# A hybrid encoder layer on one core: grouped FFN-up products, a quarter-wise opening, another VectorE order at the output projection, and 14 zero products on TensorE

## The chip, the cores and the metric

One core of a Trainium2 chip runs the whole program. The metric is device time in microseconds. Three runs of the kernel before gave 1219.9, 1220.18 and 1221.23 us, so its median is 1220.18 us.

## What is computed

One layer (`DEPTH = 1`) over 256 tokens of width 2048, everything in f32:

```python
h = x
u = rmsnorm(h, norm_mix)
p_mla, p_ssm, p_swa = split(u @ w_in)                       # 2048 -> 3660
h = h + concat([mla_mixer(p_mla), mamba2_mixer(p_ssm), swa_mixer(p_swa)]) @ w_out   # 2048 x 2048
q = rmsnorm(h, norm_cross) @ cross_wq                       # 4 heads of 128
k, v = rmsnorm(mem, norm_mem) @ cross_wkv                   # 256 memory tokens, 2048 -> 1024
h = h + softmax(q k^T / sqrt(128)) v @ cross_wo
g, val = split(causal_dwconv(rmsnorm(h, norm_ffn) @ ffn_w_up))   # 2048 -> 2 x 5632
h = h + (silu(g) * val) @ ffn_w_down                        # 5632 -> 2048
return rmsnorm(h, norm_final)
```

## The kernel before

**Products.** A weight slab is 1 MB: 128 partitions by 2048 f32 columns. SyncE loads it into one of three slots of `raw`; ScalarE rounds it into `hi` (the helper `split`, L382); VectorE takes the rest `lo = raw - hi` (L775); TensorE then works in fp32r. The activations have the same two parts, `ux[:, k, 0]` = `uh` and `ux[:, k, 1]` = `ul`. A product is three passes: hi by uh, hi by ul, lo by uh (`three`, L1326 to L1331, 256 or 512 columns each). In the FFN-up product (`wide_product`) the first two are one matmul of 512 columns, since `uh` and `ul` of a k lie side by side:

```python
pe.matmul(bank[b][:, :], wh, both_, start=(k == 0), stop=False)      # L1353, 512 columns
pe.matmul(bank[b][:, 0:T], wl, uh[:, k, :], start=False, stop=False) # L1354, 256 columns
```

for 16 values of k; the last k has them in the other order (L1356, L1357). A tile waits for `lo_ready` of its slab, which VectorE gives.

**Order.** It is written out by hand on every engine, with semaphores between them; the slabs are numbered (`N_XK` 0 to 3 the keys' weights, `N_XV` 4 to 7 the values', then `w_in`, `N_OUT` 41 to 56, `N_WQ`, `N_WO`, `N_FFN` from 65). On each engine the code for slab n is followed by the `split` of slab n+2.

**The opening.** `mem` comes in four loads of 512 columns, and the key weights as four slabs of one head each, (2048 rows by 128 columns: 512-byte rows in DRAM). SyncE waits for all four quarters of `mem` before it issues slabs 1 to 3, then 15 loads of vectors and tables, x (two loads of 1 MB), the positions, four small parameter loads, and the value slabs. TensorE turns `mem` by transposes (`turn_group`, L1377: 8 groups of 4), ScalarE and VectorE scale the turned groups into `uh` and `ul` (`token_hi` L430, `token_lo` L817), and TensorE makes the four key tiles one after the other (48 matmuls of 256 columns each), then the four value products. Behind each value product it turns two groups of x (`turn_scaled`, L1396), for which it needs `x_diag`, the root of x's squares. VectorE takes each key when it is done (`take_key`, L904) and makes the rotary angles (L919 to L938, 19 operations that wait for one another) after the last key.

**The output projection.** 16 slabs; the product of slab `N_OUT` (41) lies in banks 2 and 3, and the product of slab `N_OUT+4` wants the same banks, so it waits until `add_mixed(N_OUT, ...)` on VectorE (L1131, signal `mix_added`) has taken them. `sum_tiles` (L824) adds the squared tiles with a `tensor_reduce` over a strided view.

**The FFN.** 11 groups of 8 up tiles and 4 down products. An up tile's bank is taken by ScalarE (`up_low`, L730) and VectorE (L1254, L1255, signal `fconv_raw`); tile c waits for `fconv_raw` of tile c-2, since banks 0 and 1 alternate. The first take also needs `hf_scale` (L1218), which VectorE copies when TensorE has spread it (`spread_scale`, L1403, signal `hf_spread`) between the first two tiles.

## Time and profile before

| | us |
|---|---|
| median of 3 runs | 1220.18 |
| the profiled execution | 1220.99 |
| its span, first to last instruction | 1219.2 |
| TensorE busy | 1187.8 (97%) |
| VectorE busy | 896.8 (74%) |
| ScalarE busy | 655.0 (54%) |
| read from HBM | 214.33 MB, 178 GB/s over the span |
| mean granted clock | 0.994 |

The profile is of one execution. "Busy" counts the instructions of an engine, not its waits; a matmul's shown length is longer than the step from its start to the next one's start, because matmuls are pipelined, so the pace is read from the starts. 1.00 of the granted clock is 2.4 GHz and 0.50 is 1.2 GHz. The 1.8 us between the span and the execution's time lie around the program.

### The profile page before, as it was taken

What the parts mean: (1) busy time and instruction counts of PE and PEld (TensorE: products, weight loads), DVE (VectorE), ACT (ScalarE), POOL (GpSimd) and SP (SyncE); (2) the same over time, 40 slices, a digit from 0 to 9 for tenths busy, and PEclk for the clock granted to TensorE, in tenths of its full rate; (3) what the DMA queues carried; (4) which work ended last, traced back from release to release, by engine and by line L of the source; (5) the groups of instructions that cost most, each with busy time, mean ns of one, the idle gap of its engine ahead of it and who ended that gap; (6) DMA issues with size and microseconds to landing.
All of it is one profiled execution on the core that took longest, in us unless ns stands there. A gap on an engine that the chain in (4) does not pass through costs nothing.

```text
span 1219.2 us, 18801 instructions
## 1 busy us (share of the span) xinstructions
PE 1187.8 (97%) x6960; PEld 1037.7 (85%) x6960; DVE 896.8 (74%) x1257; ACT 655.0 (54%) x866; POOL 0.2 (0%) x4
## 2 busy tenths in 40 slices
PE   6899999999999999999999999999999999999996
PEld 6799999988878978888888888888888888888885
DVE  6753998778676667877767767777777677777777
ACT  6544764475644557545555555555454555555454
POOL 0000000000000000000000000000000000000000
PEclk9999999999999999999999999999999999999998
DMA  9676766432565445675765758575757657575751
GB/s 278 231 170 173 184 162 173 126 108 70 207 207 173 144 153 158 202 207 173 198 181 173 204 162 217 172 206 172 206 172 198 180 175 203 164 215 172 207 173 70
DMA packets 309358, 217.11 MB, mean 178 GB/s; under 512 B 11350, under 2 KB 272190, under 8 KB 308670
## 3 DMA queue, kind: packets, MB, share of 16 engines
q1 hardware_dynamic: 309134, 216.31, 60.8%
q8 instruction: 33, 0.54, 0.2%
q10 hardware_dynamic: 176, 0.14, 0.1%
q14 instruction: 15, 0.12, 0.0%
HBM read 214.33 MB, written 2.10 MB: 178 GB/s over the span
## 4 chain that ended last, share of the span: by engine, by line
PE 91%; DVE 3%; ACT 2%; DMA 1%; SPq 1%; issue 1%; ACTq 0%; DVEq 0%
PE bank L1353 25%; PE bank L1354 13%; PE bank L1326 9%; PE bank L1328 9%; PE bank L1327 9%; PE bank L1329 6%; PE bank L1330 6%; PE bank L1331 6%; PE bank L1357 2%; PE bank L1435 1%; DVE lo L775 1%; ACT hi L382 1%; PE bank L1466 1%; PE bank L1356 1%; DMA raw<-in_cross_wkv_dram 1%
## 5 line engine op out<-in xcount | busy, mean ns | idle before, releaser
L775 DVE TENSOR_TENSOR lo<-raw,hi 128x2048 fp32r<-128x2048 f32 x195 | 446.6, 2290 | 135.4 <-ACT hi L382 127.6
L1353 PE MATMUL bank<-ux,hi 128*128 128x512 f32 x1320 | 470.1, 399 | 1.3 <-DVE arena L1255 1.3
L382 ACT CAST hi<-raw 128x2048 fp32r<-128x2048 f32 x195 | 371.5, 1910 | 112.2 <-PE bank L1328 104.0
L1354 PE MATMUL bank<-ux,lo 128*128 128x256 f32 x1320 | 370.7, 281 | 0.0
L1353 PEld LDWEIGHTS bank<-ux,hi 128*128 128x128 f32 x1320 | 248.1, 188 | 59.0 <-issue 1.6
L1354 PEld LDWEIGHTS bank<-ux,lo 128*128 128x128 f32 x1320 | 249.3, 189 | 4.0
L1326 PE MATMUL bank<-hi,ch 128*128 128x512 f32 x464 | 181.4, 391 | 1.4 <-DVE cl L1193 1.4
L1328 PE MATMUL bank<-hi,cl 128*128 128x512 f32 x464 | 180.2, 388 | 0.0
L1327 PE MATMUL bank<-lo,ch 128*128 128x512 f32 x464 | 180.1, 388 | 0.0
L1329 PE MATMUL bank<-ux,hi 128*128 128x256 f32 (+1 forms) x592 | 170.5, 288 | 2.8 <-DVE lo L775 2.6
L1330 PE MATMUL bank<-ux,hi 128*128 128x256 f32 (+1 forms) x592 | 167.4, 283 | 0.0
L1331 PE MATMUL bank<-ux,lo 128*128 128x256 f32 (+1 forms) x592 | 167.3, 283 | 0.0
L730 ACT COPY arena<-bank 128x256 f32<-128x256 f32 x88 | 32.9, 374 | 210.2 <-PE bank L1357 210.2
L1329 PEld LDWEIGHTS bank<-ux,hi 128*128 128x128 f32 (+1 forms) x592 | 112.6, 190 | 6.5 <-DVE lo L775 2.8
L1330 PEld LDWEIGHTS bank<-ux,hi 128*128 128x128 f32 (+1 forms) x592 | 112.7, 190 | 0.1
L1331 PEld LDWEIGHTS bank<-ux,lo 128*128 128x128 f32 (+1 forms) x592 | 112.7, 190 | 0.0
L1326 PEld LDWEIGHTS bank<-hi,ch 128*128 128x128 f32 x464 | 87.1, 188 | 19.3 <-DVE cl L1193 1.8
L1234 DVE SCALAR_TENSOR_TENSOR arena<-arena,vecs 128x255 f32<-128x255 f32 (+1 forms) x176 | 85.1, 484 | 24.4 <-DVE arena L1234 3.6
L1328 PEld LDWEIGHTS bank<-hi,cl 128*128 128x128 f32 x464 | 87.1, 188 | 18.1
L1327 PEld LDWEIGHTS bank<-lo,ch 128*128 128x128 f32 x464 | 87.2, 188 | 17.8
L1254 DVE TENSOR_TENSOR arena<-bank,arena 128x256 f32<-128x256 f32 x88 | 37.2, 423 | 64.2 <-ACT arena L730 63.5
L1170 DVE TENSOR_TENSOR arena<-arena,bank 128x512 f32<-128x512 f32 x96 | 61.0, 682 | 0.7 <-PE bank L1328 0.7
(239 smaller groups left out, 1060.5 us busy)
## 6 DMA issues: line engine op xcount, KB each, us to landing
raw<-in_ffn_w_up_dram SPq DMA_DIRECT2D x88, 1024.0 KB, 5.8
raw<-in_ffn_w_down_dram SPq DMA_DIRECT2D x44, 1024.0 KB, 5.1
raw<-in_w_in_dram SPq DMA_DIRECT2D x28, 1024.0 KB, 5.6
raw<-in_w_out_dram SPq DMA_DIRECT2D x16, 1024.0 KB, 5.2
raw<-in_cross_wkv_dram SPq DMA_DIRECT2D x7, 1024.0 KB, 8.8
arena<-in_x_dram SPq DMA_DIRECT2D x4, 1024.0 KB, 5.9
raw<-in_cross_wq_dram SPq DMA_DIRECT2D x4, 1024.0 KB, 5.4
raw<-in_cross_wo_dram SPq DMA_DIRECT2D x4, 1024.0 KB, 5.1
```

What stands on the lines that cost most here:

```text
L382: a.mark(act.copy(hi[:, n % RING, :], raw[:, n % RING, :]), S("hi_ready"))
L775: d.mark(dve.tensor_tensor(lo[:, n % RING, :], raw[:, n % RING, :], hi[:, n % RING, :].bitcast(F32), ALU.subtract), S("lo_ready"))
L1170: d.mark(dve.tensor_tensor(hres[:, t, cb * 512:(cb + 1) * 512], hres[:, t, cb * 512:(cb + 1) * 512], bank[b][:, :], ALU.add), signal)
L1234: go(dve.scalar_tensor_tensor(out=cacc[:, s, tap:T], in0=craw[:, s, 0:T - tap], scalar=vecs[:, bass.ds(col, 1)], in1=cacc[:, s, tap:T], op ...
L1326: pe.matmul(dst, xh, wh, start=start, stop=False)
L1327: pe.matmul(dst, xh, wl, start=False, stop=False)
L1328: return pe.matmul(dst, xl, wh, start=False, stop=stop)
L1329: pe.matmul(dst, wh, xh, start=start, stop=False)
L1330: pe.matmul(dst, wh, xl, start=False, stop=False)
L1331: return pe.matmul(dst, wl, xh, start=False, stop=stop)
L1353: pe.matmul(bank[b][:, :], wh, both_, start=(k == 0), stop=False)
L1354: pe.matmul(bank[b][:, 0:T], wl, uh[:, k, :], start=False, stop=False)
```

## The change

**FFN up.** `wide_product` now makes all 512-column matmuls of its k range first and then all 256-column ones, and waits for `hi_ready` ahead of the first group and for `lo_ready` only ahead of the second. The matmuls are the same in number and shape.

**The opening.** The key weights come as four slabs of four k by 512 columns (2048-byte rows), each cut to a quarter of `mem`. SyncE interleaves them with the quarters of `mem` and no longer waits for `mem`; the positions go ahead of x. TensorE turns a quarter of `mem` ahead of each quarter of the product and adds to four banks, one for each head; the spread of mem's root comes behind the last quarter. `KEY_BANKS` is gone, and `X_BANKS` and the banks of the turned `mem` change. VectorE takes no key until all are done, and makes the angles right behind the `split` of slab 4, ahead of x's squares, the keys and the `split` of slab 5.

**Zero products.** VectorE clears a tile `warm` (128 by 128), and TensorE makes 14 f32 products of it by itself into bank 0 before it waits for anything.

**Output projection.** VectorE makes the low part of the MLA heads ahead of the sum of the SSM squares, and `add_mixed(N_OUT, ...)` one step earlier, right behind the heads' root. `sum_tiles` adds by halves with `tensor_tensor`.

**Start of the FFN.** VectorE copies `hf_scale` before the `split` of slab `N_FFN+2`, not behind it.

```diff
@@ SyncE
-            for q in range(4):
-                sp.dma_start(mems[:, :, q * 512:(q + 1) * 512], ...)
-                if q % 2:
...
-            for q in range(4):
-                sp.wait_ge(S(f"mem_landed{q}").sem, 16)
-            load(1, rows(cross_wkv)[:, :, P:2 * P], (KD, P))
-            load(2, rows(cross_wkv)[:, :, 2 * P:3 * P], (KD, P))
-            raw_free(3)
-            load(3, rows(cross_wkv)[:, :, 3 * P:4 * P], (KD, P))
+            load_mem(0)
+            for half in range(2):
+                sp.dma_start(raw[:, 0, half * CH // 2:(half + 1) * CH // 2].rearrange("p (a b) -> p a b", b=512),
+                             rows(cross_wkv)[:, 2 * half:2 * half + 2, 0:512])...
+            for q in (1, 2):
+                load_mem(q)
+                load(q, rows(cross_wkv)[:, 4 * q:4 * q + 4, 0:512], (4, 512))
+            load_mem(3)
...
@@ VectorE, opening
             diagonal("mem", mem_diag)
             go(dve.tensor_copy(mem_r[:, :], small[:, s_r:s_r + 2]))
-            split(3)
-            dve.wait_ge(S("mem_spread").sem, 1)
-            go(dve.tensor_copy(mem_scale, bank[4][:, 0:T]))
-            dve.wait_ge(S("x_landed").sem, 32)
-            take_key(0)
-            tile_squares("x", xs)
-            token_rsqrt("x")
-            diagonal("x", x_diag)
-            take_key(1)
             split(4)
-            take_key(2)
-            split(5)
-            take_key(3)
...
+            dve.wait_ge(S("x_landed").sem, 32)
+            tile_squares("x", xs)
+            token_rsqrt("x")
+            diagonal("x", x_diag)
+            dve.wait_ge(S("mem_spread").sem, 1)
+            go(dve.tensor_copy(mem_scale, bank[7][:, 0:T]))
+            dve.wait_ge(S("products_done").sem, products(3))
+            for j in range(X_H):
+                d.mark(dve.tensor_tensor(kxT[:, j, :], bank[j][:, 0:T], mem_scale, ALU.mult), S("key_taken"))
+            split(5)
@@ TensorE, opening
+            pe.wait_ge(S("warm_ready").sem, 1)
+            for _ in range(14):
+                pe.matmul(bank[0][:, 0:P], warm, warm, start=True, stop=True)
...
+            turn_mem(0)
+            for q in range(4):
+                if q < 3:
+                    turn_mem(q + 1)
...
+                    for j in range(X_H):
+                        o = k * 512 + j * P
+                        last = three(bank[j][:, 0:T], hi[:, q % RING, o:o + P], lo[:, q % RING, o:o + P], ...)
+            spread_scale("mem", mem_diag, 7)
             for n in range(N_XV, N_XV + 4):
...
                 if g == 0:
-                    pe.wait_ge(S("key_taken").sem, 2)
+                    pe.wait_ge(S("key_taken").sem, 1)
@@ VectorE, output projection
-            sum_tiles("ssm", sq_ssm, 6, sum_ssm)
-            mixed_var("heads", ((0, 512), (2, 768)), 0)
+            feature_lo("mla", o_mla, 6, uh[:, 10:16, :], ul[:, 10:16, :], V_MLA)
+            mixed_var("heads", ((0, 512), (2, 768)), 0)
+            sum_tiles("ssm", sq_ssm, 6, sum_ssm)
...
                 if n == N_OUT + 1:
+                    mixed_rsqrt("heads", ((0, 512), (2, 768)))
+                    dve.wait_ge(S("residual_landed").sem, 32)
+                    add_mixed(N_OUT, 1, 0, 0)
                     mixed_var("ssm", ((4, 768),), 1)
-                    feature_lo("mla", o_mla, 6, uh[:, 10:16, :], ul[:, 10:16, :], V_MLA)
-                    mixed_rsqrt("heads", ((0, 512), (2, 768)))
                 if n == N_OUT + 2:
                     mixed_rsqrt("ssm", ((4, 768),))
-                    dve.wait_ge(S("residual_landed").sem, 32)
-                    add_mixed(N_OUT, 1, 0, 0)
                     add_mixed(N_OUT + 1, 2, 1, 0)
@@ TensorE, FFN up
-            def wide_product(n, b, ks=(0, KD)):
+            def wide_product(n, b, ks=(0, KD), i=None):
...
+                pe.wait_ge(S("hi_ready").sem, turn + n + 1)
                 for k in range(*ks):
-                    wh, wl = hi[:, s, k * P:(k + 1) * P], lo[:, s, k * P:(k + 1) * P]
...
+                    pe.matmul(bank[b][:, :], hi[:, s, k * P:(k + 1) * P], ux[:, k, :, :]..., start=(k == 0), stop=False)
+                pe.wait_ge(S("lo_ready").sem, turn + n + 1)
+                for k in range(*ks):
+                    last = pe.matmul(bank[b][:, 0:T], lo[:, s, k * P:(k + 1) * P], uh[:, k, :], ...)
```

VectorE in the opening, before, from the last step of x's root (L789) and x's diagonal (L812) on. L904 takes a key, L775 is the `split` of slab 4 and then of slab 5, L919 is the first operation of the angles.

```order
L789 TENSOR_TENSOR small<-small 128x2
L812 TENSOR_SCALAR arena<-tab,small 128x128 x2
L904 TENSOR_TENSOR arena<-bank,arena 128x256
L775 TENSOR_TENSOR lo<-raw,hi 128x2048
L904 TENSOR_TENSOR arena<-bank,arena 128x256
L775 TENSOR_TENSOR lo<-raw,hi 128x2048
L904 TENSOR_TENSOR arena<-bank,arena 128x256
L919 CAST arena<-arena 128x256
```

And after the change, right behind the last operation of the angles (L926): L803 to L813 are x's squares, root and diagonal, L932 copies mem's scale, L935 takes the four keys, and the two L776 are the `split` of slabs 5 and 6.

```order
L803 ISA arena,small<-arena 128x2048
L803 ISA small 128x1
L796 TENSOR_SCALAR small<-small 128x2
L798 RECIPROCAL small<-small 128x2
L787 TENSOR_TENSOR small<-small 128x2
L788 TENSOR_TENSOR small<-small 128x2
L789 TENSOR_SCALAR small<-small 128x2
L790 TENSOR_TENSOR small<-small 128x2
L813 TENSOR_SCALAR arena<-tab,small 128x128 x2
L932 COPY arena<-bank 128x256
L935 TENSOR_TENSOR arena<-bank,arena 128x256 x4
L776 TENSOR_TENSOR lo<-raw,hi 128x2048 x2
```

The diagonal of x (L812, now L813) stood ahead of the angles and now stands behind them, and so does the `split` of slab 5.

VectorE in the output projection, before, from the `split` of slab `N_OUT+4` (L775) to the four `add_mixed` of slabs `N_OUT` and `N_OUT+1` (L1131 x4):

```order
L775 TENSOR_TENSOR lo<-raw,hi 128x2048
L1123 RECIPROCAL mixed<-mixed 128x2
L786 TENSOR_TENSOR mixed<-mixed 128x2
L787 TENSOR_TENSOR mixed<-mixed 128x2
L788 TENSOR_SCALAR mixed<-mixed 128x2
L789 TENSOR_TENSOR mixed<-mixed 128x2
L1131 SCALAR_TENSOR_TENSOR arena<-bank,mixed,arena 128x512 x4
```

After the change, from the low part of the MLA heads (L848) over the sum of the SSM squares (L829 to L832), the `split` of slab `N_OUT+3` (L776) and the heads' root to the two `add_mixed` of slab `N_OUT` (L1130 x2):

```order
L848 SCALAR_TENSOR_TENSOR ux<-arena,vecs,ux 128x256 x6
L1114 TENSOR_SCALAR mixed<-bank 128x2 x2
L829 TENSOR_TENSOR arena<-arena 128x768
L831 TENSOR_TENSOR arena<-arena 128x256
L832 TENSOR_TENSOR arena<-arena 128x256
L776 TENSOR_TENSOR lo<-raw,hi 128x2048
L1122 RECIPROCAL mixed<-mixed 128x4
L787 TENSOR_TENSOR mixed<-mixed 128x4
L788 TENSOR_TENSOR mixed<-mixed 128x4
L789 TENSOR_SCALAR mixed<-mixed 128x4
L790 TENSOR_TENSOR mixed<-mixed 128x4
L1130 SCALAR_TENSOR_TENSOR arena<-bank,mixed,arena 128x512 x2
```

The take of the product of `N_OUT` moved from behind the `split` of slab `N_OUT+4` and the second root to the place right behind the first root.

VectorE at the start of the FFN, before (L775 the `split` of slab `N_FFN+2`, L1218 the copy of `hf_scale`, L1254 and L1255 the take of the first tile):

```order
L812 TENSOR_SCALAR arena<-tab,small 128x128 x2
L775 TENSOR_TENSOR lo<-raw,hi 128x2048
L1218 COPY arena<-bank 128x256
L1254 TENSOR_TENSOR arena<-bank,arena 128x256
L1255 TENSOR_TENSOR arena<-arena 128x256
```

and after:

```order
L813 TENSOR_SCALAR arena<-tab,small 128x128 x2
L1216 COPY arena<-bank 128x256
L776 TENSOR_TENSOR lo<-raw,hi 128x2048
L1253 TENSOR_TENSOR arena<-bank,arena 128x256
L1254 TENSOR_TENSOR arena<-arena 128x256
```

The copy and the `split` have changed places.

## Rows read from the trace of the kernel before

**Rows 1.** TensorE's waits, whole run: line, releaser, us in total, times, longest
```profile
PE bank L1326 <- DVE lo L775: 3.2, 1, 3.2
PE bank L1326 <- DVE arena L1131: 2.8, 1, 2.8
PE bank L1329 <- DVE lo L775: 2.6, 1, 2.6
```

**Rows 2.** By stretch: length; busy PE, PEld, DVE, ACT, POOL; clock; DMA share; GB/s
```profile
17.00:20.50 3.50, 1.67 (x14) 1.47 (x13) 1.55 (x1) 3.49 (x2) 0.00 (x0) 1.00 1.19 292
39.50:42.50 3.00, 0.51 (x5) 0.30 (x3) 1.62 (x1) 1.35 (x1) 0.00 (x0) 1.00 1.03 383
43.98:47.39 3.41, 3.41 (x9) 2.65 (x9) 2.73 (x3) 2.54 (x2) 0.00 (x0) 0.50 0.82 280
337.50:340.90 3.40, 3.40 (x10) 2.63 (x9) 3.40 (x4) 1.22 (x1) 0.00 (x0) 0.50 0.51 198
```

**Rows 3.** Timeline: start, length, line, op, shapes [idle <-releaser]; TensorE's first transposes
```profile
5.87 3.67 PE L1377 MATMUL bank<-tab,arena 128*128 128x128 f32 x16
10.04 1.10 PE L1377 MATMUL bank<-tab,arena 128*128 128x128 f32 x8 [0.49 <-DMA arena<-in_mem_dram]
```

**Rows 4.** Timeline of ScalarE, the first value slab
```profile
38.95 1.90 ACT L382 CAST hi<-raw 128x2048 fp32r<-128x2048 f32 x1 [1.58 <-DMA raw<-in_cross_wkv_dram]
```

**Rows 5.** Timeline, VectorE in the opening: x's squares and root, a key, the angles
```profile
33.75 2.28 DVE L802 CUSTOM_DVE_ANT_0 arena<-arena 128x2048 f32<-128x2048 f32 x1
...
36.96 0.17 DVE L795 TENSOR_SCALAR small<-small 128x2 f32<-128x2 f32 x1 [0.92 <-ACT arena L514]
...
38.85 0.42 DVE L904 TENSOR_TENSOR arena<-bank,arena 128x256 f32<-128x256 f32 x1
...
47.20 0.28 DVE L919 CAST arena<-arena 128x256 f32<-128x256 int32 x1
...
54.48 0.29 DVE L938 TENSOR_SCALAR arena<-arena 128x256 f32<-128x256 f32 x1
```

**Rows 6.** Chain that ended last: the turn of x
```profile
50.56 1.79 PE bank L1396 x16
```

**Rows 7.** Timeline of VectorE, output projection
```profile
322.69 2.98 DVE L824 TENSOR_REDUCE arena<-arena 128x256 f32<-128x1536 f32 x1 [1.63 <-ACT arena L435]
...
325.84 2.29 DVE L775 TENSOR_TENSOR lo<-raw,hi 128x2048 fp32r<-128x2048 f32 x1
...
329.02 2.46 DVE L840 SCALAR_TENSOR_TENSOR ux<-arena,vecs,ux 128x256 fp32r<-128x256 f32 x6
...
335.60 2.73 DVE L1131 SCALAR_TENSOR_TENSOR arena<-bank,mixed,arena 128x512 f32<-128x512 f32 x4
```

**Rows 8.** Timeline of VectorE, start of the FFN
```profile
481.42 0.42 DVE L1218 COPY arena<-bank 128x256 f32<-128x256 f32 x1
```

**Rows 9.** Timeline of TensorE, start of the FFN
```profile
480.17 0.61 PE L1403 MATMUL bank<-arena,tab 128*128 128x128 f32 x4
...
483.46 0.47 PE L1353 MATMUL bank<-ux,hi 128*128 128x512 f32 x1 [1.28 <-DVE arena L1255]
```

**Rows 10.** Timeline, TensorE, one FFN-up tile
```profile
561.73 0.40 PE L1353 MATMUL bank<-ux,hi 128*128 128x512 f32 x1
...
567.02 0.28 PE L1356 MATMUL bank<-ux,lo 128*128 128x256 f32 x1
567.14 0.40 PE L1357 MATMUL bank<-ux,hi 128*128 128x512 f32 x1
567.38 0.40 PE L1353 MATMUL bank<-ux,hi 128*128 128x512 f32 x1
```

**Rows 11.** Timeline, TensorE, down product and next tile; 15 steps in the gap
```profile
602.71 0.39 PE L1326 MATMUL bank<-hi,ch 128*128 128x512 f32 x1
...
606.11 0.39 PE L1353 MATMUL bank<-ux,hi 128*128 128x512 f32 x1
606.33 0.28 PE L1354 MATMUL bank<-ux,lo 128*128 128x256 f32 x1
```

More of the change, by code:

```diff
@@ L875, in attend_norm @@
                     d.mark(ins, S("probs_ready") if t == 1 else step)
+            d.mark(dve.memset(warm, 0.0), S("warm_ready"))
             dve.wait_ge(S("vecs_ready").sem, 1)
-            for g in range(4):
-                token_lo("mem", g, V_MEM, g)
             dve.wait_ge(S("first_hi").sem, 1)
@@ L883, in _ @@
                    S("first_lo"))
-            for g in (4, 5):
-                token_lo("mem", g, V_MEM, g)
+            for g in (0, 1):
+                token_lo("mem", g, V_MEM, mem_bank(g))
             dve.wait_ge(S("hi_ready").sem, 1)
@@ L888, in _ @@
                    S("lo_ready"))
-            for g in (6, 7):
-                token_lo("mem", g, V_MEM, g)
-            split(1)
+            for q in (1, 2, 3):
+                for g in (2 * q, 2 * q + 1):
+                    token_lo("mem", g, V_MEM, mem_bank(g))
+                split(q)
             tile_squares("mem", mems)
-            split(2)
             token_rsqrt("mem")
@@ L1481, in _, with turn_mem @@
-            for n in range(N_XK, N_XK + 4):
-                if n == 0:
+            def turn_mem(q):
+                pe.wait_ge(S(f"mem_landed{q}").sem, 16)
+                for g in (2 * q, 2 * q + 1):
+                    if g == 3:
+                        pe.wait_ge(S("vecs_ready").sem, 1)
+                    if g >= 4:
+                        pe.wait_ge(S("mem_lo").sem, 2 * (g - 4) + 2)
+                    turn_group("mem", mems, g, mem_bank(g))
+            turn_mem(0)
+            for q in range(4):
+                if q < 3:
+                    turn_mem(q + 1)
+                if q == 0:
@@ new lines, in _ @@
+                for k in range(4):
+                    if k == 2:
+                        if q == 0:
+                            ready(0)
+                        if q == 3:
+                            pe.wait_ge(S("vectors_landed").sem, N_VECTORS)
+                            for m, (r, col) in enumerate(((V_ROWS_A, 0), (40, V_CW), (88, V_FW), (88, V_FW + 88), (88, V_FW + 176), (88, V_FB))):
+                                last = pe.transpose(bank[6][:, col:col + r], vrows[0:r, m, :], tab[0:r, C_ID:C_ID + r])
+                            last.then_inc(S("vecs_turned").sem, 1)
+                    kk_ = 4 * q + k
+                    pe.wait_ge(S("mem_lo").sem, 2 * (kk_ // 2) + 2)
+                    for j in range(X_H):
+                        o = k * 512 + j * P
+                        last = three(bank[j][:, 0:T], hi[:, q % RING, o:o + P], lo[:, q % RING, o:o + P], uh[:, kk_, :], ul[:, kk_, :],
+                                     kk_ == 0, kk_ == KD - 1)
@@ L1496, in _ @@
+                last.then_inc(done, 1)
+            spread_scale("mem", mem_diag, 7)
             for n in range(N_XV, N_XV + 4):
@@ L1842, in z_bank, with mem_bank @@
     return n % 3 if n < N_U else (n - N_ZB + 1) % 3
+def mem_bank(g):
+    return 4 + g % 4
 def hx_bank(g):
```

98 lines of the change are left out of this document (41 added, 57 removed).

## The prediction

> **What bounds the kernel now.** I read the shares of busy time first: TensorE 97%, VectorE 74%, ScalarE 54%. The reader is to see that only two things can move the end: TensorE's pace, and its few waits. The list of waits comes next. Besides the start, whose end is at 5.87 us [rows 3], it has three of over 2 us [rows 1]: 3.2 us before the first value product (`lo` of slab 4), 2.8 us for `mix_added`, and 2.6 us for `lo` of slab 1; and one of 1.28 us at the third FFN-up tile [rows 9]. The windows give a price behind a wait: after the 3.2 and the 2.8 us the granted clock stood at 0.50, the lower level, for 3.4 us [rows 2], which costs 3.4/2 = 1.7 us each; the stretch around the 2.6-us wait shows 1.00. Last, the timelines of TensorE and VectorE at the four places of the change. The rest of the span is one unbroken run of matmuls, so what is won or lost early reaches the end in full.
>
> The sum is made against the profiled execution, 1220.99 us (span 1219.2), 0.8 above the median of the runs, 1220.18.
>
> **FFN-up tiles.** One tile takes 561.73 to 567.38 = 5.65 us [rows 10] for 16 pairs of a 512- and a 256-column matmul: 0.353 a pair. Behind a 256-column one, the 512-column one takes 0.24 to the next start (567.14 to 567.38), 0.353 - 0.117 = 0.236 more exactly. In the down product, where 512 follows 512, 15 steps take 602.71 to 606.11 = 3.40, so 0.227 each; and the wide form's own matmul behind one of these takes 606.33 - 606.11 = 0.22 as well [rows 11], so the width of its moving operand is not what makes it slow. A 256 behind a 256 takes 0.12 (567.02 to 567.14). The new tile: 0.236 for the first 512, 0.233 for one more, between the two, as the run sets in, 14 x 0.2267 = 3.174, then 0.117 + 15 x 0.120 = 1.917: 5.560, so 0.089 less than today's 5.649 (16 x 0.353). There are 11 x 8 = 88 tiles; the first two lie ahead of the wait at the third, which hides them. 86 x 0.089 = **-7.65 us**. `lo` is now wanted 16 x 0.23 = 3.7 us later than before, so no wait is added; but the last tiles leave banks to be taken at the same places as before, so none goes either, and there was none. Bounds: nothing changes, 0; if 512 ran at the 0.22 of the single row, 86 x 16 x 0.016 = 22 us, for which no run of rows speaks. By the Trainium skill ("TensorE: Matmul & The Clock Gate", Back-to-back issue gap) an isolated matmul's gap depends on its columns alone, N/2.4 + 2.5 ns, so the order would be worth nothing; the rows differ from it, 236 against 227 ns for the same 512 columns.
>
> **Output projection.** VectorE's work of today: a strided sum 2.98 us, a `split` at 325.84, the low part of the heads 2.46, a root (it ends at 335.60), four adds in 2.73 [rows 7]. New order: the low part stands ahead of the second sum; the sum by halves over 768 + 256 + 256 columns I put at 1.9 (by 256 columns at 0.42 [rows 5], 768 at about 0.42 x 3 less its fixed part). The second sum starts when ScalarE's squares are there, 322.69, or a little after: 324.7. The `split` of `N_OUT+3` starts no later than today, 325.84, and ends at 328.1; the five small steps of the root, 1.0; the two adds, 2.73/2 = 1.4: **`mix_added` at 330.5**. TensorE wants it when it stops now, 337.16 - 2.76 = 334.2. The `split` of `N_OUT+4` (2.3, behind a 0.2 step) then ends at 333.0, 1.2 ahead of need, so the next in line is late by nothing; the one after ends about 337.7 against a need of 339.3. The wait of 2.8 us goes, and with it the 1.7 of the low clock: **-4.5 us**. Bounds: -4.5, and 0 if something equally late stands behind it (as a rival below).
>
> **Opening.** DMA first. In the window with 512-byte rows the queues bring 292 GB/s, with 2048-byte rows 383 [rows 2]. 4.2 MB of key weights then take 10.9 us, not 14.4: 3.4 less; and slabs 1 to 3 no longer wait for `mem`, of which I count 2.5 us. The first value slab, which lands at 38.95 [rows 4], lands at about 33 (35.5 if only the rate counts; 28 if all 9.4 MB ahead of it run at 383 GB/s without a pause). Cast and `split` take 43.23 - 38.95 = 4.3, so **slab 4 is ready at 37.6** on VectorE, not at 43.2 (its end is the start of the product after the 3.2-us wait). The keys, which end at 40.0 now (43.2 - 3.2), start about 2 us earlier and have no 2.6-us wait, but wait for the quarters of `mem`: they end at 37 to 38.4. The first value product runs 38 to 43.4 (24 x 0.227 = 5.4) and at the full clock, since the gap ahead of it is short.
>
> Then the new order bites. The turn of x needs `x_diag` and the first key taken. Behind the end of `split` 4 VectorE makes the angles (47.20 to 54.8, 7.6), x's squares (2.3), root and diagonal (36.96 to 38.85, 1.9), the copy of mem's scale and one key (0.4 each) [rows 5]: 37.6 + 12.6 = 50.2, with the signals **50.7**. TensorE stands from 43.4 to 50.7, **7.3 us**, where it had its 3.2-us wait before. It comes back at the low clock: the turn of x takes 1.79 at the full clock [rows 6], 3.4 to 3.6 at the low: 54.2. Meanwhile VectorE takes three keys (1.1) and splits slab 5 (2.3): 54.1. The second value product starts at **54.0**, before at 50.56 + 1.79 = 52.35 [rows 6]. So what the DMA wins, and the low clock behind the old wait, is more than eaten: **+1.5 us** (I take 0.2 off for the clock's return within the turn). Bounds: +0.5 (slab 4 ready at 36.6) to +3.8 (slab lands at 35.5). Behind it the `split` of slab 6 follows at once, ready near 56.5, and the product of slab 5 ends near 59.5: no wait.
>
> The zero products: the sixteen transposes at 5.87 take 3.67 us, 0.23 each [rows 3]; 14 like them 3.2 us, at the low clock 6.4. TensorE is empty till 5.87 and waits for `mem` once more after these transposes (0.49 [rows 3]); cost 0, at most 1. They may keep the clock up; the transposes already ran at 0.23, so there is nothing to win. The spread of mem's root is moved, not changed.
>
> **Start of the FFN.** VectorE now waits for `hf_spread` ahead of the `split`. TensorE spreads at 480.17 to 480.53 [rows 9]; the copy (0.42 [rows 8]) starts at 480.7 and is done at 481.1, the `split` at 483.3 to 483.4. Now TensorE starts 483.46 - 481.42 = 2.04 us after the copy starts, so some 1.65 after it is done; the same behind the `split` gives 485.0, and I take 484.8, since the loop's own start, part of these 1.65, may run beside the `split`. Before: 483.46. **+1.35 us**, bounds 0 and +1.6. The wait grows from 1.3 to 2.7-3.0 us, between the 2.6 that kept the clock and the 2.8 that lost it: 0 to 1.7, I take **+0.8**.
>
> **Sum.** -7.65 - 4.5 + 1.5 + 1.35 + 0.8 = -8.5: 1220.99 - 8.5 = **1212.5 us**, 7.7 below the median.
>
> **The rivals.** (a) *Slower: the 0.236 is the price of the wide operand, not of the change of width.* `uh` and `ul` of one k are read by a matmul of two 256-column blocks; in a run of them none gets the rest that a 256 gives, and each keeps 0.236 or more, while the single 0.22 was the doing of the matmul ahead of it. Then a tile takes 16 x 0.236 + 16 x 0.120 = 5.70, 0.045 more than now: 86 x 0.045 = +3.9 in place of -7.65, sum 1220.99 + 3.9 - 4.5 + 3.65 = **1224.0**. It decides from a tile of 5.67 on. For it: no run of such matmuls is in the trace. Against it: the 0.22 of rows 11, which stands at every group's start. 5%. (b) *The order of the matmuls is worth nothing,* tile 5.65: 1220.99 - 4.5 + 3.65 = **1220.1**, no change; 5%. It is also what the skill's rule gives. (c) *The value slab lands at 36,* since more rows of other loads are brought ahead of it: `split` 4 at 40.3, everything behind it 2.7 later: **1215.2**, 17%. (d) *Another wait takes the place of `mix_added`:* the heads' root waits for the last squares, or slab `N_OUT+5` is late; 1.3 us of the 4.5 come back: **1213.8**, 10%. (e) *The opening wins:* the first value product waits less and the angles fill the slack; with `split` 4 at 34 the gap is no longer and the second product starts at 34 + 12.6 + 0.5 + 3.5 = 50.6, 3.4 earlier than forecast: **1209.1**, 5%. The forecast has 58%.
>
> **How the numbers follow.** 0.2% is 2.4 us, about what a measurement of this kernel can tell from no change: faster is below 1217.7. Forecast, (c), (d) and (e) lie there, 90%; (b) is the 5% of no change, (a) the 5% slower. The range leaves out (a) and (b) and the far ends of the others: from a little under (e), 1208.5, for an FFN start that keeps its clock, to 1217, which is (c) with the lost clock at the FFN in full (+0.9) and a further 0.9 of late DMA.
>
> **What would show it.** FFN-up tile start to start 5.56 us with steps of 0.227; 5.65 is (b), 5.70 is (a). No wait of TensorE for `mix_added` at 334, clock 1.00 at 337. A cast of the first value slab at 33; the wait of TensorE for the first key 7 us long, ending near 50.7, with the clock at 0.50 behind it; the second value product at 54. At the FFN a wait of about 3 us for `fconv_raw`, ending near 484.8 less what was won before. The forecast falls if a tile takes over 5.62, or if the sum up to the FFN (-4.5 + 1.5 = -3.0) is off by more than 3 us.

## The result, and the profile after

The changed kernel takes 1212.62 us (median of 4 runs, 1211.70 to 1214.16) against 1220.70 before (4 runs, 1219.90 to 1222.51): a ratio of 0.9933 with a 95% interval of 0.9916 to 0.9950. The forecast was 1212.5 in 1208.5 to 1217.0. The profiled execution of the changed kernel took 1211.85 us, its span is 1210.0; that of before had 1220.99 and 1219.2. The spans differ by 9.2 us, the medians by 8.1: the profiled execution lies at the low end of its four (1211.70, 1211.85, 1213.39, 1214.16), and what may set the others apart is told under "The clock behind short gaps".

The list of TensorE's waits of the changed kernel, against [rows 1] (line, what released it, us in total, times, longest):

```profile
PE bank L1396 <- DVE arena L935: 6.6, 1, 6.6
PE bank L1377 <- DMA arena<-in_mem_dram: 2.4, 1, 2.4
PE bank L1351 <- DVE arena L1254: 2.2, 1, 2.2
...
PE bank L1409 <- DVE lo L776: 1.1, 1, 1.1
```

The waits for `lo` of slab 4 and slab 1 and for `mix_added` are gone, as argued. The wait for the first key is there at 6.6 us (7.3 forecast), and the one at the third FFN-up tile has grown from 1.28 to 2.25. One was not forecast at its place: 1.15 us at the output projection, for the `split` of slab `N_OUT+3`.

The opening on TensorE and VectorE (timelines), against [rows 4 to 6]:

```profile
36.86 0.47 PE L1325 MATMUL bank<-hi,ux 128*128 128x512 f32 x1
...
49.21 3.78 PE L1396 MATMUL bank<-arena 128*128 128x128 f32 x16 [6.63 <-DVE arena L935]
52.64 0.77 PE L1325 MATMUL bank<-hi,ux 128*128 128x512 f32 x1
```
```profile
34.23 2.29 DVE L776 TENSOR_TENSOR lo<-raw,hi 128x2048 fp32r<-128x2048 f32 x1 [0.23 <-DVE mem_r L903]
36.45 0.28 DVE L907 CAST arena<-arena 128x256 f32<-128x256 int32 x1
...
43.72 0.29 DVE L926 TENSOR_SCALAR arena<-arena 128x256 f32<-128x256 f32 x1
...
47.88 0.48 DVE L813 TENSOR_SCALAR arena<-tab,small 128x128 f32<-128x128 f32 x2
...
48.73 1.42 DVE L935 TENSOR_TENSOR arena<-bank,arena 128x256 f32<-128x256 f32 x4
```

ScalarE's cast of the first value slab, and the loads' rate in a stretch of 2048-byte rows:

```profile
32.26 1.89 ACT L386 CAST hi<-raw 128x2048 fp32r<-128x2048 f32 x1
```
```profile
10.20:13.20 3.00, 3.00 (x27) 3.00 (x28) 3.00 (x7) 2.77 (x6) 0.00 (x0) 1.00 1.05 408
```

The queues bring 408 GB/s here, against 292 with the 512-byte rows [rows 2], and the cast at 32.26 no longer waits for its slab, as it did at 38.95. `split` 4 ends at 36.5 (37.6 forecast), the angles at 44.0, and the first key is taken at 48.73 to 49.1. The first turn of x takes 3.4 us to the next product, 52.64 - 49.21, at the low clock. The second turn, in the timelines before and after:

```profile
57.66 1.95 PE L1396 MATMUL bank<-arena 128*128 128x128 f32 x16
```
```profile
58.50 1.95 PE L1396 MATMUL bank<-arena 128*128 128x128 f32 x16
```

The chain of [rows 6] puts such a start 0.16 us later than the timeline does (57.82 for 57.66), so both sides are taken from the timeline here.

The stretches by clock (columns as in [rows 2]): the turn of x, where `mix_added` was missed before, and what follows the third tile's wait.

```profile
49.21:52.64 3.43, 3.43 (x16) 3.43 (x17) 3.43 (x5) 2.59 (x3) 0.00 (x0) 0.50 0.00 0
334.00:338.00 4.00, 4.00 (x19) 3.32 (x18) 3.83 (x9) 2.13 (x5) 0.00 (x0) 1.00 0.61 188
481.60:485.00 3.40, 3.40 (x15) 2.84 (x16) 3.26 (x4) 2.95 (x4) 0.00 (x0) 1.00 0.87 254
```

The output projection: ScalarE's cast of slab `N_OUT+3`, VectorE's `split` of it and the take, and TensorE's new wait.

```profile
325.94 1.91 ACT L386 CAST hi<-raw 128x2048 fp32r<-128x2048 f32 x1 [3.59 <-DMA raw<-in_w_out_dram]
```
```profile
327.88 2.29 DVE L776 TENSOR_TENSOR lo<-raw,hi 128x2048 fp32r<-128x2048 f32 x1 [2.51 <-ACT hi L386]
...
331.10 1.41 DVE L1130 SCALAR_TENSOR_TENSOR arena<-bank,mixed,arena 128x512 f32<-128x512 f32 x2
```
```profile
330.23 0.61 PE L1409 MATMUL bank<-tab,arena 128*128 128x1 f32 x4 [1.15 <-DVE lo L776]
```

The slab lands 1.3 us later, against what runs beside it, than before: from TensorE's pause near 265 us to this cast it is 325.94 - 266.27 = 59.7 us, before 323.77 - 265.43 = 58.3. VectorE waits 2.51 us for its cast, and TensorE 1.15 for VectorE. The take of the product of `N_OUT` then ends at 332.5 (330.5 forecast); that is before TensorE's need, so the wait of 2.8 us and the low clock behind it are gone all the same.

The FFN, against [rows 8 to 10]: VectorE and TensorE at its start, and two up tiles.

```profile
478.00 0.42 DVE L1216 COPY arena<-bank 128x256 f32<-128x256 f32 x1 [3.19 <-PE bank L1403]
478.46 2.29 DVE L776 TENSOR_TENSOR lo<-raw,hi 128x2048 fp32r<-128x2048 f32 x1
480.67 0.42 DVE L1253 TENSOR_TENSOR arena<-bank,arena 128x256 f32<-128x256 f32 x1
```
```profile
477.36 0.61 PE L1403 MATMUL bank<-arena,tab 128*128 128x128 f32 x4
...
481.60 3.91 PE L1351 MATMUL bank<-ux,hi 128*128 128x512 f32 x16 [2.25 <-DVE arena L1254]
```
```profile
553.55 3.82 PE L1351 MATMUL bank<-ux,hi 128*128 128x512 f32 x16
...
559.12 3.82 PE L1351 MATMUL bank<-ux,hi 128*128 128x512 f32 x16
...
564.68 0.63 PE L1351 MATMUL bank<-ux,hi 128*128 128x512 f32 x2
```

A tile takes 559.12 - 553.55 = 5.57 us, the next 564.68 - 559.12 = 5.56.

Where the time went, from places that both traces have (start times in the span, in us):

| place | before | after | difference |
|---|---|---|---|
| second turn of x | 57.66 | 58.50 | +0.8 |
| spread of `hf`'s root (behind opening and projection) | 480.17 | 477.36 | -2.8 |
| third FFN-up tile | 483.46 | 481.60 | -1.9 |
| end of the span | 1219.2 | 1210.0 | -9.2 |

So the opening costs 0.8, the stretch with the projection wins 3.65, the start of the FFN costs 0.95, and the other tiles win 7.3.

### The profile page after: what moved, and what is told of

Same layout as the page of the kernel before. It is cut to its first block, busy times and chain, and to the rows that moved or that the text cites. A ratio compares the mean times of both kernels' runs of the same rounds, so it can differ in the third digit from the quotient of the medians.

```text
span 1210.0 us, 18869 instructions
## 1 busy us (share of the span) xinstructions
PE 1181.7 (98%) x6988; PEld 1042.4 (86%) x6988; DVE 892.3 (74%) x1264; ACT 654.5 (54%) x866; POOL 0.2 (0%) x4
## 4 chain that ended last, share of the span: by engine, by line
PE 91%; DVE 4%; ACT 2%; DMA 2%; issue 1%; SPq 0%; ACTq 0%; DVEq 0%
PE bank L1351 26%; PE bank L1355 14%; PE bank L1325 9%; PE bank L1326 9%; PE bank L1327 9%; PE bank L1328 6%; PE bank L1330 6%; PE bank L1329 6%; PE bank L1435 1%; ACT hi L386 1%; DVE lo L776 1%; PE bank L1466 1%; DMA raw<-in_w_out_dram 1%; PE bank L1396 1%; DMA arena<-in_mem_dram 1%
## 5 line engine op out<-in xcount | busy, mean ns | idle before, releaser
L776 DVE TENSOR_TENSOR lo<-raw,hi 128x2048 fp32r<-128x2048 f32 x195 | 446.4, 2289 | 133.6 <-ACT hi L386 125.8
L1351 PE MATMUL bank<-ux,hi 128*128 128x512 f32 x1408 | 336.5, 391 | 2.2 <-DVE arena L1254 2.2
L1351 PEld LDWEIGHTS bank<-ux,hi 128*128 128x128 f32 x1408 | 259.2, 188 | 52.8 <-DVE arena L1254 2.4
L1355 PEld LDWEIGHTS bank<-ux,lo 128*128 128x128 f32 x1408 | 180.9, 191 | 7.1
L1355 PE MATMUL bank<-ux,lo 128*128 128x256 f32 x1408 | 183.1, 283 | 0.0
L719 ACT ACTIVATE arena<-arena,vecs 128x256 f32<-128x256 f32 x88 | 53.0, 603 | 15.9 <-DVE arena L1254 15.9
```

The costliest lines, as they stand in the source:

```text
L719: a.mark(act.activation(cacc[:, s, :], craw[:, s, :], ACT.Identity, scale=vecs[:, bass.ds(tile + (V_FW + 2 * 2 * FT), 1)], bias=vecs[:, ba ...
L776: d.mark(dve.tensor_tensor(lo[:, n % RING, :], raw[:, n % RING, :], hi[:, n % RING, :].bitcast(F32), ALU.subtract), S("lo_ready"))
L1351: pe.matmul(bank[b][:, :], hi[:, s, k * P:(k + 1) * P], ux[:, k, :, :].rearrange("p a b -> p (a b)"), start=(k == 0), stop=False)
L1355: last = pe.matmul(bank[b][:, 0:T], lo[:, s, k * P:(k + 1) * P], uh[:, k, :], start=False, stop=(k == KD - 1))
```

## The experiments

Each was run beside the kernel before, on the same chip; a ratio is to that kernel, with its 95% interval. The chips differ between groups of experiments (before: 1221.56 us for experiments 1 to 4, 1220.52 for 5, 6, 7 and 9, 1221.74 for 8, 10, 11 and 12; 1220.70 for the changed kernel), so kernels of different groups are compared by their ratios, or inside their traces.

**1. The grouped FFN products alone,** on the kernel before.

```diff
-  for k: pe.matmul(512 columns, hi of k); pe.matmul(256 columns, lo of k)
+  for k: pe.matmul(512 columns, hi of k)
+  pe.wait_ge(lo_ready)
+  for k: pe.matmul(256 columns, lo of k)
```

> The kernel before with the grouped wide_product alone. Theory (a 512-column matmul behind a 256-column one costs 9 ns more, a 256-column one behind a 512-column one 3 ns less, so ungrouping costs 15 times 6 ns a tile): FFN-up tiles 0.09 us shorter, 7.3 to 7.7 us less than before, 1213; waits at the opening, at mix_added and at the third tile stay as they were (3.2, 2.8, 1.3 us). Rival (the gain in the FFN comes from lo being wanted later, not from the steps): the steps stay 236 and 117 ns and the idle time of TensorE in the FFN falls instead; since the FFN of the kernel before shows no idle time, that would give 0 to 1 us.

Measured: 1214.13 us against 1221.56, ratio 0.9935 (0.9921 to 0.9949). The third tile starts at 483.90 and the span ends at 1212.3, 728.4 us for what took 1219.2 - 483.46 = 735.7: -7.3. The waits of the opening and the projection stayed (3.8, 3.0 and 2.8 us, before 3.2, 2.6 and 2.8). TensorE has no idle time in the FFN to lose, so the gain is in the steps, as the theory has it.

**2. VectorE's new order at the output projection alone,** on the kernel before with the sums by halves.

```diff
+            feature_lo("mla", ...)
             mixed_var("heads", ...)
+            sum_tiles("ssm", ...)
             n == N_OUT + 1:  split
+                mixed_rsqrt("heads", ...); add_mixed(N_OUT, 1, 0, 0)
                 mixed_var("ssm", ...)
-                feature_lo("mla", ...); mixed_rsqrt("heads", ...)
             n == N_OUT + 2:  split; mixed_rsqrt("ssm", ...)
-                add_mixed(N_OUT, 1, 0, 0)
```

> The kernel before with VectorE's new order and the sums by halves at the output projection alone. Theory (the 2.8 us wait and 1.7 us of low clock go, and a 1.15 us wait for the split of slab N_OUT+3 comes, since that slab lands late behind the residual loads): 3.4 to 4.5 us less than before, 1216.5. Which of the two ends shows whether the late slab belongs to the new order or to the luck of one execution. Rival (the late slab comes from the new order, whose VectorE no longer frees the slot as early): the cast of N_OUT+3 is later than 323.8 by 1 us or more here too.

Measured: 1215.83 us, ratio 0.9956 (0.9940 to 0.9971); span 1212.9. The cast of slab `N_OUT+3`:

```profile
322.65 1.91 ACT L382 CAST hi<-raw 128x2048 fp32r<-128x2048 f32 x1 [2.25 <-DMA raw<-in_w_out_dram]
```

From a place just ahead of the projection (the only TensorE pause near 265) to the one behind it (near 450) this kernel takes 264.32 to 444.35 = 180.0 us, the kernel before 265.43 to 450.29 = 184.9: **-4.8**, and no new wait. So the new order is worth the forecast 4.5 and a little more, and the late slab does not come from it; the rival falls.

**3. The new opening alone** with its zero products, all else as before.

```diff
-            load_mem(0..3); keys' weights by heads, 512-byte rows; 4 key tiles one after the other
+            load_mem(q); keys' weights by quarters, 2048-byte rows; 4 key tiles side by side
-            split(3), x's squares and diagonal, keys, split(4), split(5), angles
+            split(4), angles, x's squares and diagonal, keys, split(5)
```

> The new opening with its zero products alone; FFN products, output projection and FFN start are as before. Theory (what the DMA wins is eaten by VectorE's order): 0.7 us more than before, 1220.9; TensorE waits 6.6 us for the first key at 42.5, and the second turn of x starts at 58.5 against 57.82. Rival (the opening as a whole is a gain and later waits took it back in the changed kernel): 1 to 2 us less than before.

Measured: 1223.92 us against 1221.56, ratio 1.0020 (1.0011 to 1.0029), the one part that makes the kernel slower. TensorE's waits:

```profile
PE bank L1388 <- DVE arena L928: 6.6, 1, 6.6
PE bank L1318 <- DVE arena L1123: 2.8, 1, 2.8
...
PE bank L1401 <- DVE lo L776: 1.3, 1, 1.3
```

The place near 265 comes at 266.09, +0.66 against before, and the stretch up to the place near 450 takes 186.2 us, **+1.3**: the wait for slab `N_OUT+3` (L1401) stands here too, with VectorE's old order. The price of 1.3 us thus came with the opening and its zero products, 270 us behind them. How they move that landing the traces do not tell: over the issues around it, the median from issue to landing of four `w_out` slabs is 11.0 us in the kernel before and in experiment 1, 11.6 in the changed kernel and 11.8 here. It stays open; experiment 6 narrows it.

**4. The old order at the start of the FFN,** in the changed kernel.

```diff
+            split(N_FFN + 2)
             dve.wait_ge(S("hf_spread").sem, 1)
             go(dve.tensor_copy(hf_scale, bank[3][:, 0:T]))
-            split(N_FFN + 2)
```

> The changed kernel with the split of N_FFN+2 put back ahead of the copy of hf_scale. Theory (the copy waits for TensorE's spread, and the split stands behind it): the wait at the third FFN-up tile falls from 2.25 to 1.3 us, so 1.0 us less than the changed kernel, about 1211.6 in time and a ratio of 0.992 to the kernel before. Rival (the split hides nothing, since the take of the first tile waits for up_low or the loop's start anyway): the wait stays 2.2 us and the time is that of the changed kernel.

Measured: 1211.63 us, ratio 0.9918 (0.9904 to 0.9931), against 0.9933 (0.9916 to 0.9950) for the changed kernel: the intervals overlap, so the times alone do not show the gain. The trace does: between the starts of neighbouring matmuls at the third tile 1.23 us pass instead of 2.52. The theory holds: the `split` had been put behind a wait for TensorE.

**5. The angles behind the keys, in three pieces,** in the changed kernel.

```diff
             split(4)
-            (angles, 19 operations)
             (x's squares, root, diagonal; mem's scale; four keys)
             split(5)
+            (angles, first 7)
             for n in range(N_XV, N_XV + 4):
                 ...
                 split(n + 2)
+                if n == N_XV: (angles, next 8)
+                if n == N_XV + 1: (angles, last 4)
```

> The changed kernel with VectorE's opening in another order: x's squares, root, diagonal, mem's scale and the four keys right behind the split of slab 4, then the split of slab 5, and the angles in three pieces behind the splits of slabs 5, 6 and 7 (ScalarE's sines and the sign one slab later). Theory (the 6.6 us wait and the low clock behind it come from the angles' place, 7.6 us ahead of x's diagonal and the keys): the first key is taken near 41.6, TensorE does not wait at 42.4, the clock stays, the second turn of x starts at 50.4 and not 58.5, and the time is 8 us less than the changed kernel, about 1204.6. Rival (VectorE has no room for the angles later, or the next slabs have not landed, so the wait comes back at the second to fourth value product): the second or third turn waits 3 to 7 us and the gain is under 3 us.

Measured: 1206.24 us, ratio 0.9879 (0.9864 to 0.9895). VectorE and TensorE in the opening:

```profile
38.08 2.28 DVE L803 CUSTOM_DVE_ANT_0 arena<-arena 128x2048 f32<-128x2048 f32 x1
...
42.76 1.42 DVE L913 TENSOR_TENSOR arena<-bank,arena 128x256 f32<-128x256 f32 x4
44.09 2.28 DVE L776 TENSOR_TENSOR lo<-raw,hi 128x2048 fp32r<-128x2048 f32 x1
```
```profile
44.06 1.95 PE L1398 MATMUL bank<-arena 128*128 128x128 f32 x16
46.43 0.50 PE L1327 MATMUL bank<-hi,ux 128*128 128x512 f32 x1 [0.42 <-DVE lo L776]
...
52.03 1.95 PE L1398 MATMUL bank<-arena 128*128 128x128 f32 x16
```

The wait of 6.6 us is gone but for 0.42, and the second turn starts at 52.03, 6.5 earlier than in the changed kernel and 5.6 earlier than before. The 1.6 us missing to the forecast 50.4 lie at 10 to 15 us, where this execution's clock stood at 0.66:

```profile
10.00:15.00 5.00, 4.86 (x28) 4.86 (x29) 4.59 (x11) 4.66 (x7) 0.00 (x0) 0.66 1.05 409
```

TensorE's waits show no other one of over 0.5 us at the value products: the rival falls. The gain that the faster loads and the earlier keys had made was there, but hidden by the place of the angles.

**6. No zero products,** in the changed kernel.

```diff
-            for _ in range(14):
-                pe.matmul(bank[0][:, 0:P], warm, warm, start=True, stop=True)
```

> The changed kernel without the zero products. Theory (they raise the clock early, but what they win lies ahead of the wait for the first key, which VectorE sets): the first transposes step by 0.21 us and not 0.11, the keys' product starts near 11 at 0.24 us a step for up to 3.4 us and ends up to 1.7 us later than 36.5, the first key is taken up to 1.7 us later or at the same time, and the time is 0 to 1.7 us more, nearest 0.3. Rival (they cost time, since they share the tensor engine or delay the first turn of mem): 0.5 to 1 us less.

Measured: 1214.65 us, ratio 0.9947 (0.9933 to 0.9961); the interval takes in the changed kernel's 0.9933. The five runs lie in two groups, 1212.0 and 1212.2, and 1214.7 to 1215.5; the trace is of the fastest. In it the `split` of slab 4 starts at 35.80, not 34.23, so the key wait does not hide what the products win: TensorE starts again at 50.78, not 49.21, and comes to the place near 265 at 267.61, 1.3 later than with the products. But the wait at slab `N_OUT+3` is missing, so the place near 450 comes at 447.61 (447.60 with them), and the span is 1210.1. The two cancel in this trace; experiment 11 has no such wait on either side and shows the products' worth.

```profile
325.94 1.91 ACT L386 CAST hi<-raw 128x2048 fp32r<-128x2048 f32 x1 [2.25 <-DMA raw<-in_w_out_dram]
```

This also narrows the question of experiment 3. From the place near 265 to this cast it is 325.94 - 267.61 = 58.3 us, as in the kernel before and in experiments 1 and 2; in the changed kernel and in experiments 3, 4, 5, 7 and 8 it is 59.7 to 59.9. The loads of the opening are the new ones here too, so they alone do not make the slab late in this one trace. The slab is late in every trace with the new opening and the zero products (and the residual at its old place), and in no other. Why stays open.

**7. Half the changes of width,** in the changed kernel.

```diff
-  512 x16, then 256 x16
+  512(k) 256(k) 256(k+1) 512(k+1) 512(k+2) 256(k+2) ...
```

> The changed kernel with the FFN-up matmuls in the order 512, 256, 256, 512, 512, 256, ... so that half of the changes of width are left, and lo is wanted at once. Theory (the price is 6 ns for each 512 that stands behind a 256, net of what the 256 behind a 512 saves): 8 of 16 changes come back, each tile is 0.045 us longer than the grouped one and the time is 3.9 us more than the changed kernel, 1216.5. Rival (the gain is that of lo being wanted later, or comes only from long runs): the whole 7.5 us comes back, 1220.

Measured: 1213.88 us, ratio 0.9943 (0.9930 to 0.9955). From the third tile (482.21) to the end of the span (1211.2) it takes 729.0 us; the changed kernel 1210.0 - 481.60 = 728.4, the kernel before 735.7. So nearly the whole gain is kept, +0.6 and not +3.9. Four matmuls, two of each width, take 0.70 us:

```profile
560.30 0.63 PE L1354 MATMUL bank<-ux,hi 128*128 128x512 f32 x2
560.77 0.39 PE L1357 MATMUL bank<-ux,lo 128*128 128x256 f32 x2
561.00 0.62 PE L1354 MATMUL bank<-ux,hi 128*128 128x512 f32 x2
```

(561.00 - 560.30.) Over the whole trace the mean steps are 233 ns from a 512 to a 256, 115 to the next 256, 116 to a 512 and 233 to the next 512: 348 ns for a 512 and a 256. Both the theory, in its size, and the rival fall. A price for each 512 behind a 256 can't be right; what is left is a price of strict alternation, or one of two neighbours that read the same k. Experiment 8 parts these.

**8. Strict alternation, but no shared k.**

```diff
-  512 x16, then 256 x16
+  512(0), 512(1), 256(0), 512(2), 256(1), ... 512(15), 256(14), 256(15)
```

> The changed kernel with strictly alternating widths, but the 256-column product one k behind the 512-column one, so that neighbours share no k. Theory (the price belongs to the strict alternation of widths; where every second change is gone, as in the order 512, 256, 256, 512, nearly all of it is): a pair takes 353 ns as in the kernel before, a tile 5.65 us, the time 7.5 us more than the changed kernel, 1220. Rival (the price belongs to two neighbours that read the same k of the activations): a pair takes 347 to 348 ns and the time stays at 1212.6 to 1213.5.

Measured: 1221.03 us, ratio 0.9998 (0.9989 to 1.0006). The whole gain is lost: from the third tile (481.96) to the end of the span (1217.7) it takes 735.8 us, as before; a pair takes 561.18 - 560.83 = 0.35 and 561.54 - 561.18 = 0.36:

```profile
560.83 0.40 PE L1354 MATMUL bank<-ux,hi 128*128 128x512 f32 x1
561.07 0.28 PE L1357 MATMUL bank<-ux,lo 128*128 128x256 f32 x1
561.18 0.40 PE L1354 MATMUL bank<-ux,hi 128*128 128x512 f32 x1
...
561.54 0.40 PE L1354 MATMUL bank<-ux,hi 128*128 128x512 f32 x1
```

The mean steps are 236 ns behind a 512 and 117 behind a 256, as in the kernel before. So the price lies in the strict alternation of the two widths, 353 ns a pair against 348 where it is broken up. Why TensorE is slower in that pattern, the traces do not show.

**9. The residual behind slab `N_OUT+3`,** in the changed kernel.

```diff
-                if m == 2:
+                if m == 3:
                     sp.wait_ge(S("out_done").sem, A_X)
                     (two loads of the residual)
```

> The changed kernel with the two loads of the residual behind the load of slab N_OUT+3, not ahead of it. Theory (TensorE waits 1.15 us at 330 since that slab lands late behind 2 MB of residual): the cast of the slab starts 4 us or more earlier, the wait goes, and the time is 1.2 us less than the changed kernel, about 1211.4. Rival (the wait only moves: the residual or slab N_OUT+4 is late now): mix_added or the next split is late by as much and the time is the same.

Measured: 1213.04 us, ratio 0.9934 (0.9921 to 0.9948): no difference in the time. In the trace the wait of 1.15 us is gone, and the place near 450 comes at 446.42, not 447.60. But behind the same 2.2-us wait at the third tile the clock fell this time:

```profile
480.46 5.42 PE L1351 MATMUL bank<-ux,hi 128*128 128x512 f32 x16 [2.24 <-DVE arena L1254]
```
```profile
480.46:484.00 3.54, 3.54 (x9) 2.82 (x10) 3.39 (x4) 3.07 (x4) 0.00 (x0) 0.55 0.88 256
```

Sixteen matmuls take 5.42 us where they took 3.91 in the changed kernel. So the theory holds for the wait, and what it won is less than one fall of the clock is worth, so six runs, from 1210.25 to 1214.27, can't show it.

**10. Three edits together,** in the changed kernel: those of experiments 4, 5 and 9.

```diff
+            split(N_FFN + 2)                      (ahead of the copy of hf_scale)
+            keys, split(5), angles in three pieces
+                if m == 3:                        (the residual)
```

> The changed kernel with three edits: VectorE's opening with the angles in three pieces behind the keys, the split of N_FFN+2 ahead of the copy of hf_scale, and the residual behind slab N_OUT+3. Theory (the three waits they take away lie apart and add up: 6.5 us, 1.0 and 1.3, and the short gap at the FFN's start keeps the clock): 1203.8, a ratio of 0.986. Rival (they meet: TensorE comes to the output projection earlier than the slabs do, so that the wait at N_OUT+3 is back): 1205.5 or more.

Measured: **1202.61 us**, ratio 0.9845 (0.9830 to 0.9859). Runs: 1201.12, 1201.19, 1202.61, 1202.70, 1202.70. The edits add up: in the traces 6.5 from experiment 5, 1.6 for the clock that fell there at 10 and stayed up here, 1.3 from experiment 4 and 1.2 for the wait at slab `N_OUT+3` make 10.6 us, and the spans differ by 1210.0 - 1199.3 = 10.7. The runs fall in two levels 1.5 us apart; the mean granted clock is 0.998 in the two of the lower and 0.996 in the three of the upper one. The trace is of a lower one.

**11. The same without zero products.**

```diff
-            for _ in range(14):
-                pe.matmul(bank[0][:, 0:P], warm, warm, start=True, stop=True)
```

> The same as the one before, without the zero products. Theory (the keys' product now reaches the end, so a low clock at its start costs its full price): the milestones behind the keys come up to 1.7 us later than in a run of the kernel before whose clock stayed up, and the same as in one whose clock fell at 10 to 15; the time is 0 to 1.7 us more, 1204.8. Rival (they are worth nothing, since in the run with them the clock fell at 10 to 15 anyway): the same time within 0.5 us.

Measured: 1203.37 us, ratio 0.9854 (0.9840 to 0.9868); runs from 1202.88 to 1203.83, all above the five of experiment 10 (highest 1202.70). The place near 265 comes at 260.01 against 258.20, so the products are worth 1.8 us where the clock then holds. The start of TensorE without the products, then with them (experiment 10):

```profile
6.12 1.97 PE L1378 MATMUL bank<-tab,arena 128*128 128x128 f32 x8
10.15 1.97 PE L1378 MATMUL bank<-tab,arena 128*128 128x128 f32 x8 [2.06 <-DMA arena<-in_mem_dram]
```
```profile
6.87 1.09 PE L1379 MATMUL bank<-tab,arena 128*128 128x128 f32 x8
10.15 1.09 PE L1379 MATMUL bank<-tab,arena 128*128 128x128 f32 x8 [2.19 <-DMA arena<-in_mem_dram]
```

Eight transposes take 1.97 us without them and 1.09 with them, at the same shown granted clock of 1.00. Without them the slow pace reaches into the keys' product: its 256-column matmuls step by 0.21 us till 13.8 and by 0.12 behind it, and the column reads 1.00 throughout.

**12. Nine more zero products** behind the turn of `mem`'s first quarter, on experiment 10.

```diff
             turn_mem(0)
+            for _ in range(9):
+                pe.matmul(bank[0][:, 0:P], warm, warm, start=True, stop=True)
```

> The kernel with the three edits and the zero products, and nine more zero products behind the turn of mem's first quarter, where TensorE waits 1.7 to 2.6 us for the second. Theory (a gap of this length sometimes costs the clock at 10 to 15, by 1.7 us): the idle time before the second quarter falls under 0.8 us, the clock at 10 to 15 is 1.00, and the median is 0.5 to 1 us below the kernel without them. Rival (nine products end behind the landing of the quarter and delay it, or the clock falls as before): the same or 0.3 us more.

Measured: **1201.15 us**, ratio 0.9836 (0.9822 to 0.9849), runs 1200.98 to 1201.22. They fill the gap:

```profile
7.15 1.09 PE L1379 MATMUL bank<-tab,arena 128*128 128x128 f32 x8
8.07 2.17 PE L1493 MATMUL bank<-arena 128*128 128x128 f32 x18
10.08 1.05 PE L1379 MATMUL bank<-tab,arena 128*128 128x128 f32 x8
```

The lower of the two levels is now the only one in five runs, where experiment 10 had it in two of five. That is what the theory says, though with so few runs luck is not shut out, and no run of the upper level was traced. Of all kernels here this is the best: 0.9836 of the kernel before, where the changed one has 0.9933.

## Why the prediction came out right, point by point

**FFN-up tiles.** Forecast 5.560 us a tile and -7.65, measured 5.56 to 5.57 and -7.3. The missing 0.3 is 4 ns a tile: the steps among the 512s average 228.3 ns (1289 of them in the trace), and the slower ones reach over the first five of a tile, where the forecast had two at 236 and 233 and the rest at 226.7. Rivals (a) and (b), a tile of 5.70 or 5.65, are out: the same matmuls take 348 or 353 ns a pair by their order. With (b) goes the use that the prediction made of the Trainium skill ("TensorE: Matmul & The Clock Gate", Back-to-back issue gap): the page gives the gap by columns alone for an isolated matmul, and says that in a stream the weight load counts too. In this stream the same 512 columns take 236 or 228 ns by their order; the measurement decides. But the reason given, that a 512 behind a 256 is the slow one, fails: with half of such neighbours left, only 0.6 us came back. The right sum came from comparing two streams, grouped and alternating; it did not show which change of order would do.

**Output projection.** Forecast -4.5, measured -3.65 from the second turn to the FFN. The two prices in it (2.8 of wait, 1.7 of clock) are right: experiment 2 has -4.8. In the changed kernel 1.3 of it is lost to slab `N_OUT+3`. The step that failed: "the `split` of `N_OUT+3` starts no later than today, 325.84"; it started at 327.88, of which 0.8 is the later opening and 1.2 the slab. Rival (d) had the size, 1.3 us, and not the place. What I had not weighed was that the slab's landing, with a margin near zero before (the `split` ended at 328.13, and TensorE came for it at 328.21), could move with another part of the change.

**Opening.** Forecast +1.5, measured +0.8. The chain of steps stands, a little early: `split` 4 at 36.5 for 37.6, which puts the first key at 49.2 for 50.7 (0.4 of this is that 0.1 and not 0.5 passes between VectorE's key and TensorE's start), at the low clock as said, and the second product at 52.64 for 54.0. Part of that is given back since the low clock reaches into the product. The slab had landed by 32.26, when ScalarE cast it without a wait, so DMA no longer set the pace; rival (c), a slab at 36, is out. The step that failed is "there is nothing to win" on the zero products: I took the 0.23 us of the first transposes for the full clock, and with the products ahead they take 0.11 each. That term, put at 0, was worth 1.3 to 1.6 us here: without the products (experiment 6) `split` 4 ends at 38.1, TensorE starts again at 50.8 and the place near 265 comes 2.2 us later than before. So the opening without them costs more than the forecast +1.5, and the forecast of 50.7 for the first key was met by the kernel that lacks them.

**Start of the FFN.** Forecast +1.35 and +0.8 for the clock. Measured +0.95 in position and no fall of the clock in the profiled execution. The +1.35 was too much by the 0.4 of pause ahead of the take: at 480.67 it follows the `split` at once. The 0.8 is a mean over two outcomes, and both occur (experiment 9). That fits a median 0.8 above the profiled execution, but the slower executions of the changed kernel were not traced. That the forecast, made against one profile of before, met the median of after is in part luck.

**The sum.** -8.5 against -9.2 from span to span: +0.3 from the tiles, +0.85 from the projection, -0.65 from the opening, -1.2 from the FFN's start. The closeness of 1212.5 to 1212.62 owes something to errors that cancel.

**The clock behind short gaps.** By TensorE's waits in the traces and the windows behind them, where the shown clock had risen before: it stayed up behind waits of 1.75 us (experiment 2, ending at 43.7), 2.25 and 2.35 (the changed kernel at 481.6 and 10.1), 2.63 (before, 21.3), 2.72 (experiment 4, 10.1) and 3.00 (experiment 1, 21.8). It fell behind 1.69 (experiment 5, 10.1), 2.24 (experiment 9, 480.5), 2.76 (before, 337.2), 2.79 (experiments 1 and 3, at 338 and 339) and 3.13 (experiment 2, 21.8).

```profile
21.76 0.39 PE L1329 MATMUL bank<-ux,hi 128*128 128x256 f32 x1 [3.00 <-DVE lo L775]
```

The falls at 10.1 and 480.5 stand at places of the code where other executions kept the clock. Between 1.7 and 3.0 us the length does not decide alone, so the prediction's line between 2.6 and 2.8 was no line; behind waits of up to 1.4 us no trace shows a fall. Each fall costs 1.5 to 1.7 us. That is about the spread of the runs of these kernels, and it was not seen in the five runs where the gap at 8 to 10 was filled.

## What to carry to other kernels

Where two engines meet at a hand-written order, ask of every long operation what stands behind it: 7.6 us of angles nobody was waiting for took all that faster loads had won, and moving them behind the keys gave 6.5 us. Do not put work that is ready behind a wait for another engine. Close gaps of TensorE of 1.7 to 3 us, or fill them where the wait can't be removed: in some executions they cost about 1.6 us more. And ask of every early gain whether a wait behind it really hides it: that of the zero products passed through the key wait, since VectorE's part of the chain started earlier too. Where a long stream mixes two widths of matmul, keep them from strict alternation, and read the gain from a measured stream, not from single steps.

## What was not expected of the hardware

Strict alternation of 512- and 256-column matmuls costs 353 ns a pair, 512, 256, 256, 512 costs 348, and runs of 16 cost 348. The granted clock reads 1.00 at the very start while eight transposes take 1.97 us instead of 1.09, and in experiment 11 till 13.8 us: there the column does not show the level, and the steps must be read. And the landing of a slab near 325 us moved by 1.3 us between traces that differ in the first 50 us, with the new opening and its zero products together and not with the new opening alone, for which no cause was found.
